# Attention inside a decoder step: the near head group in natural token order with a softmax maximum of its own and a merge per head pair, and the decode rows' key loads on ScalarE's queue

## What is computed

```python
# z = RMSNorm(x) @ w_in -> q | k | v (12 heads x 64) | u | v_sg | gate_a | gate_b
# 3 head groups of 4 heads, (window, dilation) = (128,1), (512,4), (2048,16)
# each query reads keys at distances 0, d, 2d, ..., window (129 keys, causal)
for gi, (win, dil) in enumerate(DIL_GROUPS):
    o, lse = _band_attn(_to_residue(qg, dil), _to_residue(kg, dil), _to_residue(vg, dil))
w = softmax(stack(lses), axis=0)          # per head slot, over the 3 groups
y = sum(w * stack(outs))                  # 4 x 64 = 256 wide
m = sigmoid(gate_a) * (y @ w_proj_attn) + sigmoid(gate_b) * (o_b @ w_proj_sg)
# the 8 decode rows do the same against a key and value cache (cache_win0..2)
```

## Time and profile before

| | |
|---|---|
| time, median of 3 runs | 1752.5 us (1741.85 to 1765.14) |
| span of the profiled execution | 1750.0 us |
| PE busy | 1637.9 us, 94% |
| DVE / ACT / POOL busy | 623.4 / 466.6 / 235.1 us |
| attention of pair 0, first score to the next stage's first product | 291.71 to 410.89 us |
| attention of pair 1, the same | 520.46 to 640.86 us |
| ga | 640.86 to 763.84 us |

### The profile page before, as it was taken

One profiled execution on the slowest core, in us unless ns is written; L12 is line 12 of the kernel. 1 busy time (PEld: TensorE's weight loads), 2 busy tenths in 40 slices (PEclk: granted clock), 3 DMA queues, 4 the chain that ended last, 5 costly groups with the idle time before them and its releaser, 6 DMA issues.

```text
span 1750.0 us, 25669 instructions
## 1 busy us (share of the span) xinstructions
PE 1637.9 (94%) x10409; PEld 1596.5 (91%) x10409; DVE 623.4 (36%) x1238; ACT 466.6 (27%) x818; POOL 235.1 (13%) x260
## 2 busy tenths in 40 slices
PE   5999999999999998988976999999999999999995
PEld 5999999989999888877975999999999999999985
DVE  7115531442024444244247223223223223223237
ACT  5225543332223221122234211220121121121132
POOL 6000001000001000024353110110010010010033
PEclk9999999999999999999997999999999999999997
DMA  5111121000112005304110111111111111111102
GB/s 181 49 44 40 37 73 51 13 24 25 49 29 72 12 10 152 100 25 133 38 36 12 49 49 49 37 49 49 49 49 49 38 49 49 40 47 49 49 13 97
DMA packets 132181, 90.31 MB, mean 52 GB/s; under 512 B 4760, under 2 KB 127408, under 8 KB 132080
## 3 DMA queue, kind: packets, MB, share of 16 engines
q1 hardware_dynamic: 131936, 88.30, 16.8%
q10 hardware_dynamic: 144, 0.52, 0.1%
HBM read 81.08 MB, written 7.73 MB: 51 GB/s over the span
## 4 chain that ended last, share of the span: by engine, by line
PE 83%; DVE 6%; issue 3%; DMA 3%; ACT 2%; POOL 2%; SPq 1%; DVEq 0%; ACTq 0%; POOLq 0%
PE bank L446 24%; PE bank L448 24%; PE bank L447 24%; PE psT L442 2%; PE bank L655 2%; PE psA L615 2%; DMA w_raw<-in_w_in 1%; PE psB L621 1%; DMA qb<-q_rows 1%; POOL m_lo L1764 1%; DVE pt L1514 1%; POOL acc L1826 1%; DVE acc L1579 1%; PE psB L760 1%; PE bank L442 1%
## 5 line engine op out<-in xcount | busy, mean ns | idle before, releaser
L446 PE MATMUL bank<-f_hi,w_hi 128*128 128x344 f32 x1056 | 341.1, 323 | 4.7 <-issue 4.7
L446 PE MATMUL bank<-h_hi,w_hi 128*128 128x344 f32 x1008 | 332.6, 330 | 10.3 <-DVE w_lo L1253 8.3
L448 PE MATMUL bank<-f_hi,w_lo 128*128 128x344 f32 x1056 | 339.0, 321 | 0.0
L447 PE MATMUL bank<-f_lo,w_hi 128*128 128x344 f32 x1056 | 338.9, 321 | 0.0
L448 PE MATMUL bank<-h_hi,w_lo 128*128 128x344 f32 x1008 | 323.2, 321 | 0.0
L447 PE MATMUL bank<-h_lo,w_hi 128*128 128x344 f32 x1008 | 323.2, 321 | 0.0
L1253 DVE TENSOR_TENSOR w_lo<-w_raw,w_hi 128x1024 fp32r<-128x1024 f32 x122 | 153.8, 1260 | 338.6 <-ACT w_hi L917 176.2
L446 PEld LDWEIGHTS bank<-f_hi,w_hi 128*128 128x128 f32 x1056 | 200.5, 190 | 5.6 <-issue 5.6
L446 PEld LDWEIGHTS bank<-h_hi,w_hi 128*128 128x128 f32 x1008 | 191.4, 190 | 12.6 <-DVE w_lo L1253 9.5
L448 PEld LDWEIGHTS bank<-f_hi,w_lo 128*128 128x128 f32 x1056 | 200.2, 190 | 0.0
L447 PEld LDWEIGHTS bank<-f_lo,w_hi 128*128 128x128 f32 x1056 | 200.1, 189 | 0.0
(11 more groups left out here) (276 smaller groups left out, 2047.7 us busy)
## 6 DMA issues: line engine op xcount, KB each, us to landing
w_raw<-in_w_in SPq DMA_DIRECT2D x42, 512.0 KB, 3.9
w_raw<-in_w_gate SPq DMA_DIRECT2D x22, 512.0 KB, 3.8
w_raw<-in_w_up SPq DMA_DIRECT2D x22, 512.0 KB, 3.8
w_raw<-in_w_down SPq DMA_DIRECT2D x22, 512.0 KB, 3.5
xin<-in_x_prompt SPq DMA_DIRECT2D x8, 512.0 KB, 7.6
w_raw<-in_w_out SPq DMA_DIRECT2D x8, 512.0 KB, 4.2
xre<-in_x_prompt SPq DMA_DIRECT2D x8, 512.0 KB, 8.4
out_y_prompt<-yt SPq DMA_DIRECT2D x8, 512.0 KB
```

Source lines behind the costliest of these rows:

```text
L446: mm(out[:, 0:TG], w_hi[par][:, ws], hi[:, k, tgc[tg]], start=first, stop=False)
L447: mm(out[:, 0:TG], w_hi[par][:, ws], lo[:, k, tgc[tg]], start=False, stop=False)
L448: return mm(out[:, 0:TG], w_lo[par][:, ws], hi[:, k, tgc[tg]], start=False, stop=last)
```

## The change

The near group leaves the residue order. `qk[:, 0]` and `qk[:, 3]` (its queries and keys) are kept in natural token order, and its tile T is the 128 tokens 128 T to 128 T + 127: its keys are 256 tokens (128 for T = 0). The other two groups keep their tile T (class T // 2, half T % 2). So near and far part of a step belong to different tokens; each has its own maximum, exp, sum and 64-column output (`st_at`, `ob`). A near part has 2 blocks instead of 4 or 5, so a step has 4 or 6 blocks (T = 0: 3) instead of 6 or 9.

The scores read the head's own 64 rows of `qk` (`hd`), heads in turn and into different PSUM banks; `qst` and POOL's copies are gone. `oturn` and `ocopy` are gone. The steps are written out in a new order: four groups of 3 gate chunks to each T. The division moves into a merge per pair, spread over the jobs of the next stage (qkv1 for pair 0, ga for pair 1): the near outputs and their maxima and sums are turned, copied, picked with stride 4 into residue order and turned back, DVE and ACT form the weights, DVE scales and adds, PE turns the sum, ACT writes `oaT`. The key, value and output tiles change with it: 37 transposes in `kv_turns` instead of 41, 26 cache stores for a pair instead of 32.

The decode rows' `kraw` and `qb` loads go from SP's queue to ACT's, two kk after each of 12 jobs of ga; SP stores the queries behind weight load 2, and issues the values behind loads 5 and 6. DVE takes 6 kk for each unit 1 to 4.

```diff
+        pr, _o = at("pr", [P, 2, 768], F32, _o)
+        prT, _o = at("prT", [P, 2, 6, P], F32, _o)
+        ob, _o = at("ob", [P, 2, 8, P], F32, _o)
+        psS = [[psA, psB], [psC, bank[2]]]
...
@@ SP, ga @@
+                if i == 2:
                     sp.wait_ge(s_nc, 5)
                     sp.dma_start(q_rows, qtok[:].rearrange("b g c -> b (g c)")).then_inc(q_out, 16)
-                if 1 <= i < 6:
-                    for kk in range(5 * i - 5, min(5 * i, 24)):
-                        load_k(kk)
+                if i in (5, 6):
+                    for kk in range(12 * i - 60, 12 * i - 48):
+                        rows, ck = cache(kk)
+                        sp.dma_start(cv[0:ck, kk, :], rows[:, 1, :]).then_inc(sv_in, 16)
...
@@ PE, attention @@
+                def scores(T):
+                    r, hh, w = T // 2, T % 2, P * (T % 2 + 1)
+                    N = 16 * pair + 2 * T
+                    if N >= 2:
+                        pe.wait_ge(at_m, N)
+                        pe.wait_ge(at_o, N - 2)
...
+                    for e in range(2):
+                        hd = slice(HD * e, HD * e + HD)
+                        mm(psS[e][0][:, 256 - n0:256], qk[hd, 0, own], qk[hd, 3, near], start=True, stop=True)
+                    for g in (1, 2):
+                        for e in range(2):
+                            hd = slice(HD * e, HD * e + HD)
+                            ins = mm(psS[e][1][:, w * (g - 1):w * g], qk[hd, g, own], qk[hd, 3 + g, 256 * r:256 * r + w],
+                                     start=True, stop=True)
...
+                def turns(T, e):
+                    N, nb = 16 * pair + 2 * T + e, blocks(T)
+                    half = len(nb) // 2
+                    pe.wait_ge(at_p, N + 1)
+                    if N:
+                        pe.wait_ge(at_c0, N)
+                        pe.wait_ge(at_c1, N)
...
+                def pv(T, e):
...
+                    pe.wait_ge(at_c0, N + 1)
+                    pe.wait_ge(at_c1, N + 1)
+                    if T < 7:
+                        pe.wait_ge(at_m, N + 3)
...
+                scores(0)
+                for T in range(8):
+                    gates(12 * T)
+                    if T < 7:
+                        scores(T + 1)
+                    gates(12 * T + 3)
+                    turns(T, 0)
+                    gates(12 * T + 6)
+                    turns(T, 1)
+                    gates(12 * T + 9)
+                    pv(T, 0)
+                    pv(T, 1)
...
+            def merge_step(pair, j, tg):
+                if (j, tg) == (0, 1):
+                    merge_near(pair)
+                elif (j, tg) == (1, 0):
+                    merge_place(pair)
+                elif (j, tg) == (2, 1):
+                    merge_out(pair)
...
@@ ACT @@
+                if kk == 0:
+                    act.wait_ge(at_pv, 32)
+                    act.wait_ge(q_out, 16)
+                if kk >= 2:
+                    act.wait_ge(s_kq, kk - 1)
+                act.dma_start(kraw[0:ck, kk % 2, :], rows[:, 0, :]).then_inc(sk_in[kk % 2], 16)
+                act.dma_start(qb[0:ck, kk % 2, :], q_rows[n:n + 1, 256 * g:256 * g + 256].broadcast_to([ck, 256])
+                              ).then_inc(sq_in[kk % 2], 16)
...
+                    if 2 <= 3 * j + tg < 14:
+                        load_k(2 * (3 * j + tg) - 4)
+                        load_k(2 * (3 * j + tg) - 3)
...
@@ DVE, attention @@
+                maxima(0, 0)
+                maxima(0, 1)
+                for T in range(8):
+                    if T:
+                        outputs(T - 1, 0)
+                        outputs(T - 1, 1)
+                    if T < 7:
+                        maxima(T + 1, 0)
+                    if T % 2:
+                        gated((12 * T + 3) // KD)
+                    copy1(T, 0)
+                    if T < 7:
+                        maxima(T + 1, 1)
+                    if T % 2 == 0:
+                        gated((12 * T + 7) // KD)
+                    copy1(T, 1)
+                    if T % 2:
+                        gated((12 * T + 11) // KD)
```

More of the change, by code:

```diff
@@ L360, in _ @@
                     store_kv(1)
[L362 to L371, removed]
             for i in range(8):
@@ L658, in oturn @@
-                def oturn(i, t):
-                    T = 8 * pair + 4 * i + t
-                    pe.wait_ge(at_o, 2 * T + 3)
-                    pe.wait_ge(at_oc, T + 1)
-                    turn(psO[:, 384:512], otok[:, t % 2, :]).then_inc(at_ot, 1)
-                def gates(i, n):
-                    for c in gate_chunks(n):
+                    if T < 7:
+                        pe.wait_ge(at_m, N + 3)
+                    near = [vtok[:, t, hd] for t in ((T - 1, T) if T else (T,))]
+                    far = [vtok[:, 8 * g + 4 * q + r, hd] for g in (1, 2) for q in range(hh + 1)]
@@ new lines, in pv, with gates @@
+                    b = 0
+                    for kind, values in enumerate((near, far)):
+                        for a, v in enumerate(values):
+                            ins = mm(psS[e][0][:, 256 + HD * kind:256 + HD * kind + HD], prT[:, e, b, :], v,
+                                     start=(a == 0), stop=(a == len(values) - 1))
+                            b += 1
+                    ins.then_inc(at_pv, 1)
+                def gates(c0):
+                    for c in range(c0, c0 + 3):
@@ L1406, in attention @@
-                with dve.Fori(0, 2) as i:
-                    st.enter(i, 4 * 2 + 4 * 4 + 4 + 4 + 8)
-                    maxima(i, 0)
-                    gated(i, 0)
-                    for n in range(1, 9):
-                        copy1(i, n - 1)
-                        if n < 8:
-                            maxima(i, n)
-                        for q in gates_done(n):
-                            gated(i, q)
-                        outputs(i, n - 1)
-                        if 2 in gates_done(n):
-                            lo_in(U, 2, i, 0)
-                        if 5 in gates_done(n):
-                            lo_in(U, 2, i, 1)
@@ new lines, in copy1, with gated @@
+                def copy1(T, e):
+                    N, nb = 16 * pair + 2 * T + e, (2 if T else 1) + 2 * (T % 2 + 1)
+                    half = nb // 2
+                    dve.wait_ge(at_t1, N + 1)
+                    if N >= 2:
+                        dve.wait_ge(at_pv, N - 1)
+                    v.tensor_copy(prT[:, e, half:nb, :], by4(psT[1])[:, 0:nb - half]).then_inc(at_c1, 1)
+                def gated(q):
+                    part = mb[:, 4 * pair + q // 3, tgc[q % 3]]
+                    dve.wait_ge(free[q % 3], M + q // 3 + 2)
+                    v.scalar_tensor_tensor(part, gt[:, q % 2, :], 1.0, part, ALU.add, ALU.mult).then_inc(at_gu, 1)
+                    if q % 3 == 2:
+                        lo_in(U, 0, 0, q // 3)
```

466 lines of the change are left out of this document (234 added, 232 removed).

## The result

| | before | after |
|---|---|---|
| time, median | 1752.5 us (1741.85 to 1765.14, 4 runs) | 1688.7 us (1688.33 to 1690.12, 4 runs) |
| ratio, 95% interval | | 0.965 [0.961, 0.969] |
| span of the profiled execution | 1750.0 us | 1687.1 us |
| start of the first score product | 291.71 | 290.42 (-1.3) |
| attention, pair 0 / pair 1 | 119.2 / 120.4 | 90.6 / 89.8 (-28.6 / -30.6) |

The differences add up to -62.9 us, the difference of the spans. Of the -30.6 of pair 1, 1.6 us are a stretch at the lower granted clock in this one trace of the kernel before: its stage takes 118.7 and 118.8 us in the other two traces that have the same attention (e0, e3). The side, faster, was right; the case with the largest chance was not the one that came.

A forecast was written before the change was run, and what follows sets the result against it. PE's own instructions bound the attention, waits add to ga; -40.6 attention, +8.6 merge, -0.8 `kv_turns`, -10.6 and -1.8 ga, +2 ACT's queue sum to -43.2: 1709.3 us, 8-in-10 range 1690 to 1732.

The forecast's parts named there:

- the case with the largest chance: Whole kernel: the forecast's own case, score products at full price, 1709.3 us, range 1702 to 1719; chance 0.42.
- What bounds the kernel: Attention lasts as long as PE's instructions (115.9 of 119.2 us busy); ga's rest is decode work and waits.
- the overlap: Rival in attention: two heads' score products run at once, 7 slots instead of 12, 1694.7 us; chance 0.32.
- DVE's order: Attention: `copy1` behind `maxima` makes PE wait in `turns(T, 1)`, 1.0 us in odd T, 0.56 in even T.
- The longer chain: Rival in attention: DVE's mark and link waits and ACT's order add 1 us per T, 1725.3 us; chance 0.13.
- The merge: PE work after each attention stage: 40 transposes a pair with switches, 4.3 us, twice +8.6.
- the rival on the other side: Attention: new waits drop PE's clock to half rate; 1800 us with half of both stages low; chance 0.05.
- -10.6: Ga: PE's waits for `w_lo` (8.3 us) and `sst` (2.3 us) both go.
- -1.8: Ga's first 11 us: the half-rate clock loss goes, blamed on PE's waits in the tail of `oturn` and `ocopy`.
- +2 for ACT's queue: Ga: key loads in ACT's stream delay `split_in` and `lo_in`; +2 us, between 0 and 9.
- the price of ACT's hold: Ga: a key-load round on ACT takes 4.3 us, three in a unit 12.9 against 11.3 us of products.
- the rival with ACT's queue as the new wait: Ga: the 10.6 us are not won or return as new `w_lo` waits, 1720 us; chance 0.08.

The follow-up runs named there:

- e0: The kernel before, unchanged, traced a second time: 1770.7 us, one of its longer executions.
- e3: The kernel before with only the decode rows' `kraw` and `qb` loads moved to ACT's queue, DVE taking them in sixes: 1745.1 us (ratio 0.998).
- e8: The kernel after with head 1's score products issued three gate chunks later than head 0's: 1709.1 us (ratio 0.977).
- e5: The kernel after with DVE's `copy1` ahead of the maxima of T + 1: median 1697.9 us, profiled execution 1677.6 us.
- e2: The kernel before with the two rounds of its attention loop written out on all engines: 1742.1 us (ratio 0.997).
- e6: The kernel after with three buffers instead of two for the decode rows' key and query loads: 1679.8 us (ratio 0.960).
- e4: The kernel after with `kraw` and `qb` loads back on SP's queue, five behind each of weight loads 2 to 6: 1698.0 us (ratio 0.976).
- e7: The kernel after with both the copy ahead of the maxima and three key and query buffers: 1667.7 us (ratio 0.953).
- e1: The kernel after with all three of head 0's score products issued before all three of head 1's: 1696.3 us (ratio 0.975).
- e10: The kernel of e5, unchanged, run and traced again: 1697.5 and 1700.5 us.

## What was right and what was wrong in the prediction, step by step

**What bounds the kernel** held: PE's own instructions in the attention, waits in ga. The reason given for ga's waits, five round trips between two weight loads on SP's queue, did not: with them taken off that queue in the old schedule (e3), 4.0 us for `w_lo` and 3.5 for `sst` are left.

**The score products: the step that failed.** The forecast wrote of them: "the nearest rows, say full price, which is my sum", and gave the overlap the smaller chance. The bounds were right, the choice between them was not. Without overlap a stage is 98.6 us by e8, against 99.5 forecast; with it 90.2. So the overlap gives 8.4 us a stage, 16.8 in both, of the 20.6 by which the time was missed. The nearest row was near in shape and dtype but not in what mattered: its products fill all rows of the array, so it could say nothing on two that share it. The rival had the mechanism and took 7 slots of 12, heads shifted by one record; the rows show 6. The Trainium skill, "TensorE: Matmul & The Clock Gate", Part 3 (packing small matmuls), says that products in distinct row groups run concurrently. This case's trace agrees, for fp32 products with their two records: 0.43 us for a pair.

**DVE's order** held, and its main wait. `maxima` lasts 1.29 and 1.02 us (1.30 and 1.03 forecast, from the earlier trace rows), and both starts behind `copy1` are within 0.07 us of the count. The wait of `pv(T, 1)` (0.26) and that of `scores` for `outputs` (0.45 in odd T) did not come: no row of the kernel after has them. By the forecast's count they are 2.4 us a stage. Against them stand waits that it did not count, 1.3 us in pair 0 and 0.5 in pair 1 (1.1 and 0.3 of it at the second call of `scores`, for the first maxima), and seven waits worth 5.9 us by e5 where it had 5.2. Together they make most of the 0.9 us between 99.5 and 98.6. The longer chain (the rival at 1725.3) did not come either.

**The merge** held: 4.5 us of PE's work in ga, and between the two attention stages +3.6 with `kv_turns` shorter by 0.4, 8.5 in all against +8.6. The clock stayed at 1.00 in both attention stages, with 14 waits of 0.5 to 0.8 us in them, so the rival on the other side did not come.

**Ga: mis-sized.** Forecast were -10.6 (both waits gone), -1.8 (half rate) and +2 for ACT's queue, -10.4 in all; idle time fell by 4.2, and the clock is 0.84 over 10 us as before, only later (654 to 664 us, behind the wait of 3.3). The reason given for the -1.8, PE's waits in the tail of `oturn` and `ocopy`, does not hold: e0, e2 and e3 have the same two waits there, 0.5 to 0.6 us, and full clock behind them; the first stretch at 1.2 GHz comes behind a later wait of ga (in e2 behind 3.1 us for `w_lo`). The step at fault is the price of ACT's hold: a round of 4.3 us, three in a unit. From the first to the last of twelve rounds the rows give 58.5 / 11 = 5.3 us (4.9 behind the merge's sum), and three are 16 us in a unit of 11.3, not 12.9. The forecast had named what would show if the merge's cover went, "about 6 us of `merge_sum`", but only on PE; it had not asked who else waits for DVE. By e6 the -10.6 and the -1.8 are all there with a third buffer: 123.0 + 4.5 - 114.4 = 13.1 us. So it is the buffer that takes the waits away; three buffers with the keys on SP's queue were not run. So the rival with ACT's queue as the new wait came for about 6 of its 10.6 us, together with the overlap: the cases were not exclusive.

Of the load's move the forecast cited the Trainium skill, "DMA: Bandwidth & Descriptors", section "Issuing engines are not separate DMA queues": another issuing engine saves only the time of issue. In the old schedule the traces agree: ga is 120.2 us with the loads on ACT (e3) and 120.4 with them on SP (e2). In the new one e4 measures 9, since there the place in the engine's order changed with it.

**The end of the kernel: not forecast.** From pa on the code is the same, and the kernel after is 6.4 us shorter there. PE stands there for 4.7 us with the cause issue in the kernel before, up to 2.3 at once, where PE's loop over the feed-forward rounds takes its next pass. Waits of PE from ga's end to the end of the kernel before, then the same in e0:

```profile
PE bank L446 <- issue: 4.7, 3, 2.3
```

```profile
PE bank L446 <- issue: 3.1, 3, 1.2
```

The four traces with the old attention (before, e0, e2, e3) have 1.0 to 4.7 us of it, and this part takes 982.5 to 986.2 us; the nine with the new one have none and take 978.9 to 980.0. Transfers of instructions fell from 80 packets to 57. e2, whose attention is written out as in the change, still has 2.6 us, so the loop that went is not the cause. In e0 the waits stand at the same three passes as in the kernel before, each shorter (0.9, 0.9 and 1.2 us against 1.1, 2.3 and 1.3), so the places belong to the program and the sizes to the execution. The cause stays open.

In sum, against -43.2: -16.8 from the overlap, -1.8 from the waits in the attention, +6.2 from ga and the merge (+6.5 and -0.3), -6.4 from the end, and -0.9 before the first score product (-1.3, of which 0.4 is `kv_turns` and was forecast). That is the -62.9 of the traces. Two misses of 6 us with opposite signs cancelled, by luck; the overlap is the miss.

## What to carry to other kernels

When two small products come to lie on different rows of the array and in different PSUM banks, as here, price them as one until a row says otherwise: the row of a single one is no bound from below. Here the order within the call mattered less (3.7 us a stage) than that no full-height products stood between the heads (10.2 us). Whether the same holds in one PSUM bank was not run. Before a load with a wait goes onto a computing engine's queue, write down what its releaser may be doing then and what stands behind it; a third buffer was worth 9 us here. Put the copy that PE waits for ahead of the reduction that it does not: 12 us (e7 against e6). By itself (e5) that edit lost the gain in most executions to the granted clock, so look at all executions and not only at the traced one.

Trace the kernel before more than once before a term is taken from it: its ga was 123.0 us in one trace and 120.4 in another with the same code there.

## What the runs showed of the hardware

- Two 64-row, 256-column fp32 products on the two halves of the array's rows start within 0.01 us of each other and take 0.43 us together; one head's three take 1.49 us alone (e8), both heads' 1.50. In e1 head 1's first product starts together with head 0's second and before its third, which both stand ahead of it in the order.
- A wait of PE costs about 0.2 us more than the table of waits gives (5.9 us for seven waits of 4.4 us in all).
- Near or behind waits of 1.5 to 3.5 us in ga, the granted clock was 0.84 over 10 us in one execution and, from 15 us behind the last wait, 0.50 for over 40 us in another of the same program, PE without a gap, at a loss of 21 us (e5, e10).
- The same code on PE took 982.5 to 986.2 us in four traces and 978.9 to 980.0 in nine others. The four have 1.0 to 4.7 us of waits for issue at a loop's passes, the nine none.
